# Layer norms of a two-block transformer kernel: where the mean's shift, the sums and the residual are made

## The reference, cut to what matters

```python
def layer_norm(x, g, b):
    xf = x.astype(jnp.float32)
    mu = jnp.mean(xf, axis=-1, keepdims=True)
    var = jnp.mean(jnp.square(xf - mu), axis=-1, keepdims=True)
    return ((xf - mu) * lax.rsqrt(var + LN_EPS) * g + b).astype(x.dtype)
...
    for l in range(DEPTH):
        h = layer_norm(ALPHA * h + 0.5 * swiglu(h, ffn1_w_up[l], ffn1_w_down[l]), ln_g[l, 0], ln_b[l, 0])
        mix = hybrid_mixer(h, ...)
        h = layer_norm(ALPHA * h + mix, ln_g[l, 1], ln_b[l, 1])
        h = layer_norm(ALPHA * h + 0.5 * swiglu(h, ffn2_w_up[l], ffn2_w_down[l]), ln_g[l, 2], ln_b[l, 2])
```

## Time and profile before

| | us |
|---|---|
| median of 3 runs | 2924.55 |
| lowest, highest | 2923.51, 2924.8 |
| profiled execution | 2924.64 |
| its span, first to last instruction | 2923.0 |
| TensorE busy | 2798.1 (96%) |
| VectorE busy | 2007.9 (69%) |
| ScalarE busy | 1644.4 (56%) |
| GpSimd busy | 719.3 (25%) |

### The profile page before, as it was taken

One profiled execution on the slowest core, in us unless ns is written; L12 is line 12 of the kernel. 1 busy time (PEld: TensorE's weight loads), 2 busy tenths in 40 slices (PEclk: granted clock), 3 DMA queues, 4 the chain that ended last, 5 costly groups with the idle time before them and its releaser, 6 DMA issues.

```text
span 2923.0 us, 68009 instructions
## 1 busy us (share of the span) xinstructions
PE 2798.1 (96%) x27992; PEld 2311.5 (79%) x27992; DVE 2007.9 (69%) x1910; ACT 1644.4 (56%) x1749; POOL 719.3 (25%) x571
## 2 busy tenths in 40 slices
PE   9999989989989999799989999989999999999998
PEld 8877778878877778587778888779798797797884
DVE  5556565555566655565765565668899999999986
ACT  5435654344446443445655445646777777777775
POOL 3324031131132221202022002013252242332432
PEclk9999999999999999899999999989999999999999
DMA  9664366656643565454467754348999999999995
GB/s 238 167 182 126 95 180 182 172 159 179 186 129 102 173 165 165 145 160 134 132 180 193 206 170 148 113 170 294 381 388 377 395 383 379 394 381 385 391 381 232
DMA packets 657514, 665.62 MB, mean 228 GB/s; under 512 B 25302, under 2 KB 513116, under 8 KB 657276
## 3 DMA queue, kind: packets, MB, share of 16 engines
q1 hardware_dynamic: 655696, 659.75, 68.6%
q0 software_dynamic: 704, 0.59, 0.3%
q10 hardware_dynamic: 876, 1.79, 0.2%
HBM read 661.01 MB, written 1.05 MB: 226 GB/s over the span
## 4 chain that ended last, share of the span: by engine, by line
PE 81%; issue 8%; DVE 5%; ACT 3%; POOLq 1%; DVEq 1%; DMA 0%; POOL 0%; ACTq 0%; SPq 0%
PE ps L1949 20%; PE ps L1950 20%; PE ps L1951 20%; PE ps L2625 3%; PE ps L2623 3%; PE ps L2624 3%; POOLq L1801 1%; PE ps L1990 1%; PE ps L1991 1%; PE ps L1996 1%; ACT w_hi L684 1%; DVE sq L1314 1%; ACT h L758 1%; PE ps L2278 1%; PE ps L2258 1%
## 5 line engine op out<-in xcount | busy, mean ns | idle before, releaser
L1949 PE MATMUL ps<-x_hi,w_hi 128*128 128x128 f16 (+2 forms) x5440 | 1233.7, 251 | 21.1 <-DVE prod L1207 12.0
L1950 PE MATMUL ps<-x_lo,w_hi 128*128 128x128 f16 (+2 forms) x5440 | 1233.1, 250 | 0.0
L1951 PE MATMUL ps<-x_hi,w_lo 128*128 128x128 f16 (+2 forms) x5440 | 1232.9, 250 | 0.0
L1192 DVE SCALAR_TENSOR_TENSOR w_lo<-w,w_hi 128x2048 f16<-128x2048 f32 (+4 forms) x338 | 693.9, 2063 | 281.1 <-ACT w_hi L684 280.0
L684 ACT ACTIVATE w_hi<-w 128x2048 f16<-128x2048 f32 (+4 forms) x338 | 563.1, 1671 | 164.9 <-PE ps L1951 140.3
L1949 PEld LDWEIGHTS ps<-x_hi,w_hi 128*128 128x128 f16 x5440 | 534.1, 98 | 80.9 <-issue 16.9
L1950 PEld LDWEIGHTS ps<-x_lo,w_hi 128*128 128x128 f16 x5440 | 534.0, 98 | 50.1
L1951 PEld LDWEIGHTS ps<-x_hi,w_lo 128*128 128x128 f16 x5440 | 534.1, 98 | 46.7
L1658 DVE SCALAR_TENSOR_TENSOR w_lo<-w,w_hi 128x2048 f16<-128x2048 f32 x224 | 543.9, 2453 | 30.1 <-ACT w_hi L1122 30.1
L1122 ACT ACTIVATE w_hi<-w 128x2048 f16<-128x2048 f32 x224 | 418.4, 1902 | 35.0 <-DMA w<-in_moe_w_gate 15.2
L1931 POOL CAST ff<-pb 128x512 f16<-128x512 f32 x56 | 140.2, 2503 | 634.3 <-DVE pb L1739 634.3
(11 more groups left out here) (369 smaller groups left out, 4402.9 us busy)
## 6 DMA issues: line engine op xcount, KB each, us to landing
w<-in_ffn_w_up SPq DMA_DIRECT2D x176, 512.0 KB, 5.0
w<-in_moe_w_gate SPq DMA_DIRECT2D x80, 1024.0 KB, 8.6
w<-in_moe_w_up SPq DMA_DIRECT2D x80, 1024.0 KB, 9.0
w<-in_moe_w_down SPq DMA_DIRECT2D x64, 1024.0 KB, 7.9
w<-in_w_in SPq DMA_DIRECT2D x112, 512.0 KB, 4.6
mix<-in_moe_w_down SPq DMA_DIRECT2D x48, 1024.0 KB, 8.1
w<-in_mix_w_in SPq DMA_DIRECT2D x64, 512.0 KB, 4.8
mix<-in_moe_w_gate SPq DMA_DIRECT2D x32, 1024.0 KB, 9.5
```

Source lines behind the costliest of these rows:

```text
L1192: vec.scalar_tensor_tensor(k.w_lo[:, s, 0:size], k.w32[:, s, 0:size], WS, k.w_hi[:, s, 0:size], ALU.mult, ALU.subtract).then_inc(k.parts_r ...
L1949: pe.matmul(acc, w_hi, x_hi, start=first, stop=False)
L1950: pe.matmul(acc, w_hi, x_lo, start=False, stop=False)
L1951: return pe.matmul(acc, w_lo, x_hi, start=False, stop=last)
```

## The change

Four things are done at once, all in the first block.

The shift is made from four chunks in every norm (EARLY = 4), behind unit 8 of a down phase. So ScalarE squares chunks 4 to 7 as they come, behind units 9, 11, 13 and 15, and GpSimd adds h4, h5 and h6 to one sum in the down norms too.

TensorE makes all sums of a down norm behind the last unit: GpSimd's sum of h4 to h6, GpSimd's sum of squares, then h7 and its square. In wo the square of chunk 4 is summed ahead of GpSimd's sum.

The left-over mean is squared by ScalarE straight from PSUM, and taken off each chunk by VectorE, from PSUM, one chunk ahead of the scaling, with a drain at each chunk's end. GpSimd takes no part in it. The opening takes seven chunks for both units together instead of five (TOGETHER_LN; in the first block).

ScalarE splits units 2 and 3 one behind the other and makes the residual later: in up phases behind the SiLU of units 0 and 1, in win behind their columns, at step 2; at the end of the block, at once.

```diff
+TOGETHER_LN = 7
...
-EARLY_DOWN, EARLY_WO = 6, 4
-SHIFT_STEP, SQUARES_STEP, SUMS_STEP = 2 * EARLY_DOWN, 2 * EARLY_DOWN + 1, 2 * KC - 2
...
+EARLY = 4
+SHIFT_STEP = 2 * EARLY
...
@@ ScalarE
         for u in range(ahead):
             take_at(phase.base)(0, u, phase.first + u, q)
+        if ahead:
+            residual(b0)
...
-            if u == SQUARES_STEP:
-                early_squares(n, EARLY_DOWN)
-            if u > SQUARES_STEP:
-                c = EARLY_DOWN + u - SQUARES_STEP - 1
+            if u == SHIFT_STEP + 1:
+                early_squares(n)
+            if u > SHIFT_STEP and u % 2 == 1:
+                c = u // 2
...
     def layer_norm(n, b0, q, following):
 
+        act.wait_ge(k.ln_rest, n + 1)
+        act.activation(k.tmp[:, 1, :], k.ps[:, 4, 0:T1], ACT.Square).then_inc(k.rest_squared, 1)
...
         split(following + 2, q, UNIT)
+        split(following + 3, q, UNIT)
+
+    def residual(b0):
+
         for c in range(KC):
             a = act.activation(k.h[:, c, :], k.sq[:, c, :], ACT.Identity, bias=k.col[:, b0 + c:b0 + c + 1])
         a.then_inc(k.h_ready, 1)
-        split(following + 3, q, UNIT)
...
+            if u == 2:
+                residual(C1["ln_b"])
             if u >= 2:
                 split(win.first + u + AHEAD, q, win.size if late < 0 else win.after[late])
...
@@ VectorE
-        vec.wait_ge(k.ln_rest, n + 1)
-        vec.tensor_copy(k.tmp[:, 0, :], k.ps[:, 4, 0:T1]).then_inc(k.rest_out, 1)
-        vec.drain()
-        vec.tensor_tensor(k.tmp[:, 1, :], k.tmp[:, 0, :], k.tmp[:, 0, :], ALU.mult)
-        vec.drain()
+        rest = k.ps[:, 4, 0:T1]
+
+        def u(c):
+            vec.tensor_tensor(k.h[:, c, :], k.h[:, c, :], rest, ALU.subtract)
+        vec.wait_ge(k.rest_squared, n + 1)
         vec.wait_ge(k.ln_var, n + 1)
         vec.tensor_tensor(k.tmp[:, 1, :], k.ps[:, 5, 0:T1], k.tmp[:, 1, :], ALU.subtract).then_inc(k.ln_spread, 1)
+        u(0)
...
         for c in range(KC + 1):
             scaled(c, t, lo, (n + 1) * KC)
+            vec.drain()
...
@@ GpSimd
+    def down_norm(n):
+        add_squares(n, 1, EARLY)
+        pool.wait_ge(k.ln_squared, n * KC + 6)
+        pool.tensor_tensor(rest, k.h[:, 4, :], k.h[:, 5, :], ALU.add)
+        add_squares(n, 4, 6)
+        pool.wait_ge(k.ln_squared, n * KC + 7)
+        pool.tensor_tensor(rest, rest, k.h[:, 6, :], ALU.add).then_inc(k.rest_summed, 1)
+        pool.tensor_tensor(ss, ss, k.sq[:, 6, :], ALU.add).then_inc(k.squares_summed, 1)
```

More of the change, by code:

```diff
@@ L687, in unit_used, with up @@
         act.wait_ge(k.unit_done, q * SLOTS + (g + 1 + SLOTS))
-    def up(phase, q, vec0, gates0, t, ahead=0):
+    def up(phase, q, vec0, gates0, t, ahead=0, b0=None):
         def take_at(base):
@@ L712, in square, with early_squares @@
         act.activation(k.sq[:, c, :], k.h[:, c, :], ACT.Square).then_inc(k.ln_squared, 1)
[L714 to L716 removed]
+    def early_squares(n):
+        for c in range(EARLY):
+            act.wait_ge(k.ln_centered, n * EARLY + c + 1)
             square(c)
@@ L1794, in pool_program, with add_squares @@
     ss, rest = k.prod[:, 0, :], k.prod[:, 1, :]
-    def add_squares(n, last):
-        for c in range(1, last):
+    def add_squares(n, first, last):
+        for c in range(first, last):
             pool.wait_ge(k.ln_squared, n * KC + (c + 1))
@@ L1971, in all_out, with opening @@
         pe.wait_ge(k.act_evac, act)
-    def opening(phase, q, evac, evac0, x_hi, x_lo, t, chunk, n_step, kc_step, late=False):
+    def opening(phase, q, evac, evac0, x_hi, x_lo, t, chunk, n_step, kc_step, late=False, both=TOGETHER):
         weights(phase.first, q)
@@ L1999, in opening @@
         chunk_high, chunk_low = chunk
-        together = 0 if late else TOGETHER
+        together = 0 if late else both
         for kc in range(together):
@@ L2019, in opening @@
         for j in range(2):
-            for kc in range(KC - 1 if late else TOGETHER, KC):
+            for kc in range(KC - 1 if late else both, KC):
                 if j == 0:
@@ L2039, in up @@
     def up(phase, q, vec0, x_hi, x_lo, t, chunk, late=False):
-        opening(phase, q, k.vec_evac, vec0, x_hi, x_lo, t, chunk, D, P, late)
+        opening(phase, q, k.vec_evac, vec0, x_hi, x_lo, t, chunk, D, P, late, TOGETHER_LN if t == T1 else TOGETHER)
         phase = behind_opening(phase)
@@ L2071, in wide @@
         if chunk is not None:
-            opening(phase, q, evac, evac0, x_hi, x_lo, t, chunk, P, 256, late)
+            opening(phase, q, evac, evac0, x_hi, x_lo, t, chunk, P, 256, late, TOGETHER_LN if t == T1 else TOGETHER)
             phase, before = behind_opening(phase), 2
@@ L2091, in add_var, with shift @@
         return pe.matmul(k.ps[:, 5, 0:T1], k.mean_w[:, :], x, start=first, stop=last)
-    def shift(n, early):
+    def shift(n):
         pe.wait_ge(k.first_summed, n + 1)
-        pe.matmul(k.ps[:, 4, 0:T1], k.first_w[:, early, :], k.tmp[:, 2, :], start=True, stop=True).then_inc(k.ln_mean, 1)
+        pe.matmul(k.ps[:, 4, 0:T1], k.first_w[:, :], k.tmp[:, 2, :], start=True, stop=True).then_inc(k.ln_mean, 1)
     def squared(n, c):
@@ L2108, in behind @@
             if u == SHIFT_STEP:
-                shift(n, 0)
-            if u == SUMS_STEP:
-                pe.wait_ge(k.vec_evac, vec0 + phase.base + 2 + KC - 1)
-                add_mean(k.h[:, KC - 2, :], first=True)
+                shift(n)
+            if u == 2 * KC - 1:
+                pe.wait_ge(k.rest_summed, n + 1)
+                add_mean(k.prod[:, 1, :], first=True)
                 pe.wait_ge(k.squares_summed, n + 1)
                 add_var(k.prod[:, 0, :], first=True)
-            if u == 2 * KC - 1:
                 pe.wait_ge(k.vec_evac, vec0 + phase.base + 2 + KC)
```

55 lines of the change are left out of this document (22 added, 33 removed).

## The result

| | before, us | after, us |
|---|---|---|
| median of 4 runs each | 2924.68 | 2888.95 |
| lowest, highest | 2923.51, 2925.21 | 2887.07, 2889.89 |
| profiled execution, span | 2924.64, 2923.0 | 2888.61, 2886.7 |
| mean granted clock | 0.979 | 0.986 |
| TensorE busy | 2798.1 | 2776.7 |

The ratio is 0.9878, its 95% interval 0.986 to 0.9895. The prediction had 2892.8 with 2885 to 2904.

A forecast was written before the change was run, and what follows sets the result against it. TensorE is busy nearly throughout, so its stalls and slow stretches around the six layer norms count. 26.9 + 4.6 + 0.6 + 4.7 - 1.9 - 2.4 - 0.7 = 31.8 us off 2924.6 gives 2892.8, range 2885 to 2904.

The forecast's parts named there:

- Part 1: Down norms, end of unit 14 to sum of h7: sums behind the last unit gain 26.9 us over four norms.
- rival (a): Wait for GpSimd returns behind the last unit, or h7's add queues behind VectorE's lo parts: 10 us, 2903; chance 0.09.
- Part 2: Sum of h7 to first scaled chunk: 5.46 us falls to 4.30, 1.16 at four norms, 4.6 us gained.
- The wo norms: Two wo norms, where the variance is last: a gain of 0.3 us each, 0.6 us in all.
- Part 3: First scaling to restart, norms 0 to 4: later residual saves 3.30, slower chunks cost 2.36; 4.7 us gained in all.
- Rival (c): VectorE's loop: drains cost more, 1.8 us a chunk, 16 us over six norms, 2909; chance 0.04.
- The win wait: Win phase: residual and split ahead of the latents' squares make TensorE lose 0.93 us, twice, 1.9 us.
- Norm 5: Residual there feeds the next block uncovered; slower chunks lose 2.36 us, making TensorE's wait longer than 16.43.
- The clock: Behind norm 2's opening TensorE stands some 3.4 us instead of 2.41, then runs slowly: 0.7 us lost, once.
- The second block: From TensorE's restart behind norm 5 to the end: predicted gain 0 us.

The follow-up runs named there:

- e1: Kernel before with one number changed: TensorE's sums of h6 and of GpSimd's squares stand behind unit 15 instead of between 14 and 15; 2897.53 us.
- e2: Changed kernel with the first two sums of a down norm put back between units 14 and 15; 2896.22 us.
- e3: Changed kernel with the residual's eight operations back between the splits of units 2 and 3, in all six norms; 2918.41 us.
- e6: Changed kernel with the latents' squares in win ahead of the residual's last five operations and the split of the weights; 2892.69 us median, runs in two heaps.
- e8: Changed kernel with the edits of e5 and e6 together; 2875.79 us.
- e4: Changed kernel with the left-over mean copied and squared by VectorE and subtracted by GpSimd as before, no drain in the loop; 2884.86 us.
- e5: As e4, on the changed kernel, but VectorE only copies the left-over mean and ScalarE squares the copy; 2879.95 us.
- e9: Changed kernel with five chunks for both units together behind a norm instead of seven; 2887.74 us.
- e7: The changed kernel run again, unaltered; 2890.9 us median.

## Why the prediction was right, and where by luck

**Part 1** was exact to 0.02 us a norm. Its two suppositions held: GpSimd is done long before (its adds take 0.77 each, since they run ahead of VectorE's lo parts and not beside them), and h7's add ends at 201.78, ahead of its sum at 202.06. VectorE's lo parts end at 200.92, before the last unit's end: rival (a) had 0.2 us of margin against it and found about that. e1 and e2 show that the gain belongs to the place of the sums or to the earlier shift, whichever comes first; the prediction named both but gave the gain to the place, which e2 corrects.

**Part 2.** Taken as 1.16 a norm, it was 1.22 to 1.27. ScalarE's square of the mean took 0.40, not 0.45, and began 0.65 behind the sum of h7, not 0.83, but it wasn't alone at the end: the square ends at 203.11, the sum of h7's square (L2094, whose end is modelled) at 203.13, and the profile names the latter as what the difference at 203.27 waited for. Which of the two is last isn't settled by 0.02 us; the chain that was added up came out 0.11 too long (4.30 against 4.19). The wo norms gained 0.59 each, not 0.3, of it 0.38 ahead of the sum of h7; the term had no working behind it.

**Part 3.** A chunk took 1.35 us where 1.34 was worked out: 0.42 to the subtraction, 0.35 to the lo part, 0.58 over the drain. The eighth scaling came 9.06 us behind the first, predicted 8.98. The Trainium skill, VectorE: DVE Perf Modes, section on the TRN2 errata, gives an operation from PSUM 120 cycles beside its elements, which by that estimate would have made 1.40 of it; the trace has 0.35 us start to start for these subtractions, not 0.41, so for operations in a row the page's figure is too long here. From the first scaling the restart behind norm 0 came at 14.37, predicted 14.27. The 0.1 us is the loop's: with the eighth scaling 2.44 later instead of 2.36, 3.30 - 2.44 leaves 0.86, and 0.85 was measured at all five norms, whatever released TensorE there (VectorE's lo part of weights, L1196, at norms 0 and 3, VectorE's product behind the SiLU, L1211, at 1, 2 and 4). e3 gives the other side of this term, 3.29 a norm where 3.30 was costed. Rival (c) fell: not only is a chunk 1.35 us, a second drain costs 0.05.

**The win wait** was predicted as 0.93 us; at layer 0 it stands in the timeline with 0.76, and TensorE is 0.92 us further behind at it than at its restart. e6 and e8 confirm it by its removal.

**Norm 5** lost 2.45 where 2.36 was worked out; its wait went from 16.43 to 17.77 us.

**The clock** was the term that failed. The step was: norm 1 stood 3.80 us and then ran slowly, norm 2 will stand 3.4, so it gets half of that, 0.7 us. The stretch at the lower clock was also read too short: the 1.53 us of the earlier trace rows are the length of the window that was asked for, while in the kernel before the clock stayed at its lower level up to 435.6, 5.7 us behind norm 1's restart:

```profile
428.80:435.60 6.80, 5.73 (x26) 3.85 (x27) 5.19 (x4) 2.61 (x4) 5.15 (x3) 0.50 0.53 147
```

In fact norm 1, whose wait fell to 3.34, had no slow stretch any more and its layer half gained 2.8 us, while norm 2 with the same wait of 3.34 got one and lost 2.7. Windows of the changed kernel, behind the restarts of norms 1 and 2:

```profile
615.14:620.80 5.66, 5.66 (x26) 3.79 (x27) 3.27 (x3) 4.86 (x9) 3.98 (x4) 0.50 0.99 278
421.29:427.00 5.71, 5.71 (x50) 4.83 (x51) 3.33 (x3) 4.84 (x9) 3.97 (x4) 1.00 1.05 292
```

Fifty matmuls in 5.71 us behind the one, 26 in 5.66 behind the other. The term was four times too small at each place, of both signs, and the two cancelled. The two mixers moved as well, apart from the win waits, by 1.3 us each, one up and one down. That the row of the table is near its forecast (-1.8 for -2.6) is luck. To price a wait by the lower clock behind another wait of like length was the wrong rule: the length of a wait does not settle here whether the clock falls.

**The second block** was predicted not to move and gained 3.2 us, most of the 4 us by which the forecast was too high. Windows from TensorE's restart behind norm 5 to the end, of the kernels before, after, e2 and e3 in this order:

```profile
1240.00:2923.00 1683.00, 1632.99 (x18534) 1361.58 (x18534) 1313.21 (x1126) 1058.85 (x951) 400.61 (x226) 0.98 0.78 276
```

```profile
1206.90:2886.70 1679.80, 1626.45 (x18534) 1357.42 (x18534) 1313.56 (x1126) 1059.40 (x951) 401.52 (x226) 0.99 0.79 277
```

```profile
1206.05:2894.40 1688.35, 1637.93 (x18534) 1364.18 (x18534) 1312.74 (x1126) 1059.12 (x951) 401.46 (x226) 0.98 0.78 275
```

```profile
1227.80:2917.90 1690.10, 1639.64 (x18534) 1365.21 (x18534) 1313.34 (x1126) 1059.11 (x951) 401.42 (x226) 0.98 0.78 275
```

The same 18534 matmuls keep TensorE busy for 1626 to 1640 us, and the length follows: 10.3 us between the shortest and the longest. Added up from the trace's record of the clock, it fell to its lower level (1.2 GHz) for 41, 27, 55 and 58 us of these four stretches, without the fall that was already on at their start and the one behind the last matmul. Over the thirteen profiles the length rises by about a third of a us for each us at the lower level, from 1679.5 us at 27 to 1690.1 at 58, and none lies over 1.3 us off that line. By it 14 us less would be worth 4.3, and 3.2 were measured. So the 3.2 us go with the clock, and no edit touches the code there; that the clock alone makes them is argued from this and not shown by a run. What in the first block decides how often the clock falls in the second isn't settled: its start lay anywhere from 1190.6 to 1240.0 us, and no rule was seen in that.

## What to carry to other kernels

Put a sum that closes a group behind the last work that doesn't need it, not between two pieces of work that are ready: here that was 27 of 36 us, had by one changed number. Or give the late engine its work sooner: e2 shows that this takes out the same wait, and that one of the two is enough. Split a change that helps by measuring it edit by edit: e4 and e5 showed that one part of it, the subtraction moved to VectorE, lost 9 us of what the others had gained (8.7 of them at the norms), and e9 that another did nothing. And before a few microseconds are given to an edit, compare stretches of the trace between the same instructions: totals of these kernels moved by 5 to 10 us with the granted clock where no instruction had changed.

## What the runs showed of the hardware

- Waits of equal length (3.34 us) in one program were followed by full clock at norm 1 and by 5.6 us at half of it at norm 2, in both profiles of that program. In the kernel before, waits of 3.80 and 3.81 us (norms 1 and 4) were followed by 5.7 and 3.4 us at half.
- The pattern of slow stretches is mostly a program's own: two profiles of the changed kernel, taken at different times, agree in every one. But single runs leave it: 2900.17 at a mean clock of 0.980 beside 2889.19 at 0.986 (e7), and 2897.4 beside 2885.0 (e6). 0.006 of mean clock went with 11 to 12.4 us.
- A drain of VectorE behind another drain cost 0.05 us.
- ScalarE's square of a 128x272 tile took 0.40 us from PSUM and 0.43 from SBUF, VectorE's 1.04 us from SBUF beside GpSimd. VectorE's operations with two SBUF inputs took 0.49 without GpSimd beside them, so most of what ScalarE's square saves is the meeting with GpSimd.
